# Hybrid and differential attention block on one core: sums over partitions spread over units of the first attention stream

## The reference, cut to what matters

```
# first block
qa = qk_norm(heads(q_a, A_HEADS), q_gain_a) * qscale
o_a = banded_gqa(qa, ka, heads(v_a, A_KV), SWA_WINDOW, rel_bias[:, :A_HEADS], sinks)
o_cmp, o_sel = nsa_cmp_sel(qb, k_cmp, v_cmp, k_sel, heads(vs, B_KV), bias_b)
o_win = banded_gqa(qb, k_win, heads(vw, B_KV), NSA_WINDOW, bias_b, None)
o_b = gb[..., 0, :] * o_cmp + gb[..., 1, :] * o_sel + gb[..., 2, :] * o_win
...
# second block, layer 0
c_act = jax.nn.silu(c)
cc_act = jax.nn.silu(c_ctx)
mod = (c_act @ ada_w[i] + ada_b[i])[:, None, :]
mod_c = (cc_act @ ada_w[i] + ada_b[i])[None, None, :]
sh1, sc1, g1, sh2, sc2, g2 = jnp.split(mod, 6, axis=-1)
csh1, csc1, cg1, csh2, csc2, cg2 = jnp.split(mod_c, 6, axis=-1)
a = rmsnorm(h, norm1[i]) * (1.0 + sc1) + sh1
ac = rmsnorm(hc, norm1[i]) * (1.0 + csc1) + csh1
```

## Time and profile before

| What | us |
|---|---|
| Median of 3 runs | 1743.03 |
| Lowest, highest | 1736.89, 1743.45 |
| Span of the profiled execution | 1739.3 |
| PE busy in the span | 1672.8 |
| DVE, ACT busy in the span | 975.8, 677.8 |
| Stage `att`, first logits to the last pair's transpose | 170.8 to 400.7 |

### The profile page before, as it was taken

One profiled execution on the slowest core, in us unless ns is written; L12 is line 12 of the kernel. 1 busy time (PEld: TensorE's weight loads), 2 busy tenths in 40 slices (PEclk: granted clock), 3 DMA queues, 4 the chain that ended last, 5 costly groups with the idle time before them and its releaser, 6 DMA issues.

```text
span 1739.3 us, 22898 instructions
## 1 busy us (share of the span) xinstructions
PE 1672.8 (96%) x8888; PEld 1393.1 (80%) x8888; DVE 975.8 (56%) x1805; ACT 677.8 (39%) x1413; POOL 61.9 (4%) x120
## 2 busy tenths in 40 slices
PE   4999999999999999999999999999999899999999
PEld 2777777777999999777888888887888788888887
DVE  4667466766777766767555554436555533333332
ACT  3334555564455555554322222223222433333221
POOL 0000000000000000000000000000000000000000
PEclk9899998999999999998999999998999999999999
DMA  8886333313223131222666665442443233333332
GB/s 309 210 244 180 99 96 98 97 25 87 54 55 104 38 110 37 86 73 56 189 179 182 192 178 153 116 122 75 130 124 97 73 97 97 97 97 97 100 113 79
DMA packets 290215, 202.02 MB, mean 116 GB/s; under 512 B 76247, under 2 KB 272072, under 8 KB 289082
## 3 DMA queue, kind: packets, MB, share of 16 engines
q1 hardware_dynamic: 266942, 133.21, 27.5%
q0 software_dynamic: 15536, 56.37, 10.7%
q10 hardware_dynamic: 7628, 10.97, 1.9%
HBM read 197.33 MB, written 5.28 MB: 116 GB/s over the span
## 4 chain that ended last, share of the span: by engine, by line
PE 88%; DVE 6%; ACT 2%; issue 2%; DMA 2%; ACTq 1%; SPq 0%; DVEq 0%
PE PS L864 13%; PE PS L866 13%; PE PS L865 13%; PE PS L848 4%; PE PS L846 4%; PE PS L847 4%; PE PS L1285 3%; PE PS L1287 3%; PE PS L1286 3%; PE PS L1335 2%; PE PS L1094 2%; PE PS L1359 2%; PE PS L1068 2%; PE PS L1347 1%; PE PS L1076 1%
## 5 line engine op out<-in xcount | busy, mean ns | idle before, releaser
L2016 DVE TENSOR_TENSOR WL<-WS,WH 128x512 fp32r<-128x512 f32 x416 | 268.0, 686 | 256.2 <-ACT WH L1508 255.7
L1508 ACT ACTIVATE WH<-WS 128x512 fp32r<-128x512 f32 x416 | 237.7, 621 | 179.1 <-PE PS L848 130.7
L864 PE MATMUL PS<-A3H,WL 128*128 128x512 f32 x672 | 262.9, 391 | 0.1
L866 PE MATMUL PS<-A3H,WH 128*128 128x512 f32 x672 | 261.7, 389 | 0.0
L865 PE MATMUL PS<-A3L,WH 128*128 128x512 f32 x672 | 261.4, 389 | 0.0
L864 PEld LDWEIGHTS PS<-A3H,WL 128*128 128x128 f32 x672 | 126.1, 188 | 30.0 <-issue 4.4
L866 PEld LDWEIGHTS PS<-A3H,WH 128*128 128x128 f32 x672 | 126.1, 188 | 26.4
L865 PEld LDWEIGHTS PS<-A3L,WH 128*128 128x128 f32 x672 | 126.2, 188 | 26.0
L846 PE MATMUL PS<-GH,WL 128*128 128x512 f32 x352 | 137.4, 390 | 0.6 <-DVE WL L2016 0.6
L848 PE MATMUL PS<-GH,WH 128*128 128x512 f32 x352 | 137.0, 389 | 0.0
L847 PE MATMUL PS<-GL,WH 128*128 128x512 f32 x352 | 137.0, 389 | 0.0
(11 more groups left out here) (363 smaller groups left out, 3429.1 us busy)
## 6 DMA issues: line engine op xcount, KB each, us to landing
AW<-in_ada_w POOLq DMA_DIRECT2D x96, 512.0 KB, 4.1
WS<-in_ffn_w_gate_up SPq DMA_DIRECT2D x88, 512.0 KB, 4.6
WS<-in_ffn_w_down SPq DMA_DIRECT2D x32, 512.0 KB, 4.2
WS<-in_sc_w_in SPq DMA_DIRECT2D x24, 512.0 KB, 4.1
AB<-in_w_ada SPq DMA_DIRECT2D x8, 1024.0 KB, 15.7
WS<-in_w_in SPq DMA_DIRECT2D x32, 256.0 KB, 4.4
WS<-in_diff_w_qkv SPq DMA_DIRECT2D x64, 128.0 KB, 2.6
WS<-in_ffn_w_down SPq DMA_DIRECT2D x16, 384.0 KB, 3.5
```

Source lines behind the costliest of these rows:

```text
L864: mm(PS[:, b, :], wl[:, k, :], hi[:, k, 0:S], start=(k == 0), stop=False)
L866: m = mm(PS[:, b, :], wh[:, k, :], hi[:, k, 0:S], start=False, stop=(k == KT - 1))
L1508: f(weights(p)[0][:, k, :], WS[:, p % 2, k, :], ACT.Copy).then_inc(w_hi, 1)
L2016: tt(lo[:, k, :], WS[:, p % 2, k, :], hi[:, k, :].bitcast(F32), ALU.subtract).then_inc(w_lo, 1)
```

## The change

The sums are dealt out. A table `SUMS_AT` says in which units how many of a sum's one-column products stand: e0 and e1 become e (16 products, four in each of units 0 to 3), g0 and g1 become g (four in each of units 44 to 47), h0 becomes h (three, three and two in units 76 to 78). The first piece takes the small bank, the last announces it, and DVE reads both halves in two instructions (`take_both`). The other users of the bank get new units. The context pieces on DVE (into AC) come two units after those into AA.

```
-SMALL_AT.update({"e0": 1, "e1": 2, "y0": 11, "y1": 19, "l0": 22, "t0": 25, "y2": 27, "w0": 33, "y3": 35, "g0": 37, "g1": 41, "c0": 54, "c1": 63, "c2": 66, "c3": 86})
-for _j in range(1, 4):
-    _b = N_A + 16 * _j
-    SMALL_AT.update({f"l{_j}": _b - 8, f"t{_j}": _b - 5, f"w{_j}": _b, f"y{3 + _j}": _b + 3})
-SMALL_AT.update({"h0": 70, "lam": 74, "y7": N_ATT})
+SMALL_AT.update({"e": 3, "y0": 10, "l0": 14, "y1": 18, "t0": 22, "y2": 26, "w0": 30, "y3": 35})
+SMALL_AT.update({"l1": 40, "t1": 43, "g": 47, "w1": 49, "y4": 52, "c0": 54})
+SMALL_AT.update({"l2": 56, "t2": 59, "c1": 61, "w2": 64, "y5": 67, "c2": 69})
+SMALL_AT.update({"l3": 72, "t3": 75, "h": 78, "w3": 80, "y6": 83, "c3": 86, "lam": 89, "y7": N_ATT})
+SUMS_AT = {"e": (1, True, {0: 4, 1: 4, 2: 4, 3: 4}), "g": (2, True, {44: 4, 45: 4, 46: 4, 47: 4}), "h": (3, False, {76: 3, 77: 3, 78: 2})}
...
+            def att_sums(v):
+
+                for name, (n, with_context, groups) in SUMS_AT.items():
+                    if v not in groups:
+                        continue
+                    first = sum(groups[w] for w in groups if w < v)
+                    if first == 0:
+                        pe.wait_ge(part_sum, sums_before(n + 1))
+                        take_small(att, att_small(name))
+                    for f in range(first, first + groups[v]):
+                        sums = AC[:, :] if f >= KT else AA[:, n % 2, :]
+                        at = f % KT * P
+                        m = mm(PS[:, SIDE, f:f + 1], sums[:, at:at + P], ONES[:, 0:1], start=True, stop=True)
+                    if v == max(groups):
+                        m.then_inc(small_done, 1)
...
                 if v:
                     weigh(v - 1)
+                att_sums(v)
                 for name in ATT_SMALLS:
-                    if SMALL_AT[name] == v:
+                    if SMALL_AT[name] == v and name not in SUMS_AT:
                         att_small_work(name)
...
+            def take_both(u, v, at):
+
+                dve.wait_ge(small_done, At("att").small(u) + 1)
+                tt(M2[:, at:at + 8], PS[:, SIDE, 0:8], VT[:, v:v + 8], ALU.add).then_inc(part_read, 1)
+                tt(MC[:, at:at + 8], PS[:, SIDE, 8:16], VT[:, v:v + 8], ALU.add).then_inc(small_free, 1)
...
                 if 4 <= v <= 32 and v % 4 == 0:
-                    add_pieces(16 + (v - 4) // 4, 17 + (v - 4) // 4)
+                    add_pieces(16 + (v - 4) // 4, 17 + (v - 4) // 4, True)
+                if 6 <= v <= 34 and v % 4 == 2:
+                    add_context_piece(16 + (v - 6) // 4)
```

More of the change, by code:

```diff
@@ L57 @@
     ("kvq", 1, 6, 6, 6, 5),
-    ("att", 1, 12, 0, 38, 6),
+    ("att", 1, 12, 0, 36, 6),
     ("w_out2", 1, 4, 0, 0, 0),
@@ L474, in hybrid_then_diff_conv @@
         part_in = [sem(f"part_in{s}") for s in range(A_SLOTS)]
-        part_sum, part_read, part_cread = sem("part_sum"), sem("part_read"), sem("part_cread")
+        part_sum, part_read = sem("part_sum"), sem("part_read")
         cs_ready, gains, rows_out, table_in = sem("cs_ready"), sem("gains"), sem("rows_out"), sem("table_in")
@@ L901, in add_part @@
                 add_up(a, u, AA[:, n % 2, :])
-            def add_context(a, u, n):
-                pe.wait_ge(part_sum, sums_before(n + 1))
-                add_up(a, u, AC[:, :])
             def add_beside(a, u, n, bank):
@@ L1135, in att_small_work @@
                 kind, j = name[0], name[1:]
[L1136 to L1146, removed]
+                if name == "lam":
                     pe.wait_ge(lam_mul, 2)
@@ L2029, in clear_squares, with add_pieces @@
                 dve.wait_ge(ss_zero, k - 1)
-            def add_pieces(first, end):
+            def add_pieces(first, end, later=False):
                 for i in range(first, end):
@@ L2045, in add_pieces, with add_context_piece @@
                         stt(sums, src, CS[:, c:c + 1], sums, ALU.mult, ALU.add).then_inc(part_sum, 1)
[L2046 to L2051, removed]
+                    if with_context and not later:
+                        add_context_piece(i)
+            def add_context_piece(i):
+                n, k = divmod(i, KT)
+                src = AW[:, i % A_SLOTS, :]
+                if k == 0:
+                    if n == 2:
+                        dve.wait_ge(small_free, At("att").small(ATT_SMALLS.index("e")) + 1)
+                    ts(AC[:, :], src, CS[:, 16:17], None, ALU.mult).then_inc(part_sum, 1)
+                else:
+                    dve.wait_ge(part_sum, sums_before(n) + 2 * k)
+                    stt(AC[:, :], src, CS[:, 16 + k:17 + k], AC[:, :], ALU.mult, ALU.add).then_inc(part_sum, 1)
             def take_part(a, u, v, dst, at, read):
@@ L2360, in att_small_taken @@
                 u = ATT_SMALLS.index(name)
[L2361 to L2369, removed]
+                if name == "e":
+                    take_both(u, V_ADAB, 0)
+                elif name == "g":
+                    take_both(u, V_ADAB + 8, 8)
+                elif name == "h":
                     take_part(att, u, V_ADAB + 16, M2, 16, part_read)
@@ L2388, in take_context @@
                 if q == 0:
-                    dve.wait_ge(part_cread, 2)
-                    dve.wait_ge(small_free, att.small(ATT_SMALLS.index("g1")) + 1)
+                    dve.wait_ge(small_free, att.small(ATT_SMALLS.index("g")) + 1)
                     stt(NS[:, :], MC[:, 8:16], 1.0, VT[:, V_N1:V_N1 + 8], ALU.add, ALU.mult).then_inc(ctx_scale, 1)
```

## The result

The changed kernel takes 1747.5 us, the median of 13 runs (1741.33 to 1755.42); beside it the kernel before takes 1741.95 (13 runs, 1736.89 to 1743.45). The ratio is 1.0036, with a 95% interval from 1.0025 to 1.0047: slower, by 5.55 us in the medians. The forecast was 1740.3, faster by 2.75. The time lies inside the range and the change is within 0.5%, but it went the other way.

What follows compares the result with a forecast made beforehand. PE, busy 96% of the span, was taken as the bound: its work, waits and clock. Terms 0.7 + 0.5 + 1.7 + 0.6 - 4.45 - 1.8 = -2.75 us gave about 1740.3, range 1733 to 1748.

Steps and rivals of the forecast that it cites:

- Units 44 to 49 ... Sum: +0.6: Stage att, units 44 to 49: g0's products 1.8, fall at 288.9 gone -1.5, w1's wait 0.3; together +0.6 us.
- no half clock in units 48 to 80: Sign that the forecast is right: PE's clock in the changed trace does not fall to half in these units.
- The first rival: Units 0 to 43: spread sums keep the clock up, no fall is left; -7.2 us, 1735.9, chance 0.18.
- g0's 1.8 us are paid here: Units 44 to 49: g0's products, four in each of four units beside g1's, cost PE 1.8 us.
- w1's 0.3: Unit 49: w1 waits for DVE's mixing of a group and two reads of g; estimated +0.3 us.
- Units 0 to 4, +0.7: e's first products wait 1.1 us for the small bank; a RAW wait of 0.39 at unit 4 goes; +0.7 us.
- Units 5 to 29, +0.5: y2, moved to unit 26, no longer fills PE while RAW is made for unit 28; l0's move costs 0; +0.5 us.
- Units 30 to 41, +1.7: f7 in unit 32 waits 2.1 us for DVE to read w0; unit 39 starts 1.7 us later.
- The rival in which DVE sets the pace from unit 32 on: f7 waits and DVE becomes the bound; 4.4 instead of 1.7 plus another fall of 1.5; +1.45 us, 1744.5, chance 0.20.
- Units 61 to 69, -4.45: c1 and c2 moved: w2's wait -1.98, y5's wait -0.97, fall at 336.7 gone -1.5; together -4.45 us.
- Units 70 to 80, -1.8: h0 leaves unit 70: fall at 350.3 goes, -1.5; its first products cover unit 77's wait, -0.3; together -1.8 us.
- The rule weighed against the trace: Skill's rule ties clock falls to PE idling; before the fall after 186.4 the trace showed PE busy 3.40 of 3.40 us.

## Why the prediction was wrong

**The step that failed is "Units 44 to 49 ... Sum: +0.6": it put the half clock behind g's dealt pieces at nothing.** In the profile the changed kernel lost 11.2 us from unit 42 to unit 53.

The fall at 288.9 did go (-1.6 by the starts of units 43 and 44). But "no half clock in units 48 to 80" does not follow. It rested on reading as: a lump makes the fall, so pieces make none. The added products show what the reading left out. Between g's pieces stood transposes, logits and `weigh`, all small products, and only in unit 47 three of 128x512; PE stood at half clock for 20.5 us while it was busy throughout. With large products behind the pieces the clock stayed at 1.00 and 4.7 us came back, although PE had more to do. Without g's products 7.2 came back, 3.8 of them their own time. Dealing a sum out did not dilute small work, as what stood around it was small too; it made a longer run of it. The first rival, no falls in units 0 to 43, had the same error and did not occur either.

The other two terms are smaller. "g0's 1.8 us are paid here" came out: in the run with g alone dealt out, g0's place gave nothing back, g1's gave 1.75, PE waited 0.25 longer ahead of unit 41, and the pieces cost 3.3. That is 1.8 net. w1's 0.3 did not come in the changed kernel's profile. There unit 53 has lost 12.8 on unit 44. With 3.3 for the pieces, an estimate taken over from the other run, some 9.5 us are left for the 20.5 us at half clock, which can lose at most 10.25. So the size in the profile is that of the clock, not of the work that moved. g dealt out alone costs 3.25 us in the median, w1's wait of 1.23 among them, and in a third of the runs 8 to 13.

**Units 0 to 4, +0.7:** the mechanism was right and the size near. e's first product waits 1.04 for ACT's LT, 1.1 was forecast; unit 5 starts 0.97 later. The fall came 6 us earlier, as long as before.

**Units 5 to 29, +0.5:** a little too small. Unit 30 is 0.95 later than unit 5 was; PE's waits for RAW are 2.7 in place of the 2.2 of the earlier trace rows, and unit 15, behind l0 in unit 14, has lost 0.9 on unit 14.

**Units 30 to 41, +1.7:** the mechanism was right and the size near. f7 waits 2.10 for DVE's OC, as forecast. w0 alone cost 1.5 in the median. In the changed kernel's profile the half clock there came to 10.2 and 3.4 us, where I had left 6.8. The rival in which DVE sets the pace from unit 32 on did not decide: in the run with the added products DVE's list is unchanged, and the time is 1.0006 of the kernel before's.

**Units 61 to 69, -4.45:** right in the changed kernel: w2 and y5 do not wait, the fall at 336.7 is gone, and unit 69 has won 5.1 on unit 64, 0.4 of it by c2's transposes, which are paid in unit 69 instead. Alone in the kernel before, the move gave only 2.1, not told from nothing, because h0 then waits 1.10 for c2's reading.

**Units 70 to 80, -1.8:** too large. Unit 80 has won 0.34 on unit 69. The fall at 350.3 went and h0's own 1.76 us came back, but with h0 gone PE waits 1.00 for an exponential in unit 72 (0.45, in unit 71, where h alone was moved), c2's transposes now stand in unit 69, and the dealt products cost 1.5 in units 76 to 78. I had asked what covers a wait, but here not what wait the removed work covers.

**Two numbers of the prediction.** 0.22 us a product is the time by starts (1.76 for eight); the record of 1.90 gives 0.24. The first rival's 2.9 for the long fall is not worked out: half of 6.8 is 3.4.

**The rule weighed against the trace.** Ahead of the 20.5 us PE was busy 3.50 of 3.50 us at 1.00, and work that was added kept the clock up. The Trainium skill, TensorE: Matmul & The Clock Gate, section Why this matters for your kernels, ties the fall to gaps in which PE idles; for this stretch the trace disagrees. Idle time stands ahead of a fall as well: before f7's, PE was busy for 2.12 of 3.70 us. But in the profile of the changed kernel with wide sums f7 waits 2.1 us too, and no fall follows, so no run here shows that the wait made it.

**What stays open.** A half clock is not there in every execution: the changed kernel's 13 runs go from 1741.33 at a mean clock of 0.981 to 1755.42 at 0.972, and a profile shows one run. By these figures the first is 66 us at half clock in the whole span, the second 98. The same page of the Trainium skill, section What's actually happening, says that the slow start of one and the same kernel differs between runs; the spread here is of that kind, though of the whole span and not of the start. Why the same pieces ran at half clock in one profile and at 1.00 in that of g alone dealt out is not shown. So the sizes of single stretches are those of one run, and only medians carry a verdict. The parts alone, in medians, give +3.25 (g), +1.5 (w0), -2.1 (c1 and c2) and -0.8 (h), and the rows +1.9 up to unit 30: 3.75 of 5.5. The rest was not taken apart. The sum joins medians of separate runs with rows of one profile. The context pieces' later place, e's pieces and the new places of the l and y were not tried alone.

## What to carry to other kernels

Before a piece of work is moved, look at whether the engine waits in the units that it leaves: what lies beside a wait is free, as g0 was, and moving it to a busy place costs its whole time. On PE, count small products as a risk to the clock together with what stands around them: spread over units that hold mostly small products, they lengthened the run of small work here; put beside large products, or made wider at the same duration, they kept the clock up here. Where runs of one kernel scatter by 14 us with the mean clock, change what moves the clock first, since it hides everything else.

## What the runs showed of the hardware

- PE held half clock for 20.5 us while it was busy for all of it (299.6 to 320.1), and for 23.9 us, busy for 22.6 of them, with g's sums dealt out over units 36 to 39.
- Sixteen more products of 128x384 made the changed kernel 4.7 us faster in the median.
- Eight fp32 products with 32 columns take 1.94 us, with one column 1.90 to 1.92; the wider ones alone made the kernel before 0.27% faster (0.16 to 0.37).
- Four one-column sums took 1.02 us at full clock and 1.81 at half, `weigh` 1.10 and 1.81.
- The same one-column sums in units 44 to 47 ran at 0.50 in one profile and at 1.00 throughout in another kernel's.
